# Mixer buffers and the first expert loads in another order, a gather in another place, and norms that take sums from their additions

## The reference

```python
h = layer_norm(x, ln_in_g, ln_in_b)
for l in range(DEPTH):                                    # DEPTH = 2
    y = token_mixers(h, l, ...)       # projections, 3 kinds of attention, gates, w_out
    h = layer_norm(ALPHA * h + y, ln_mix_g[l], ln_mix_b[l])
    if l % 2 == 0:
        y = swiglu(h, w_gate_dense, w_up_dense, w_down_dense)       # D_FF = 3584
    else:
        y = moe_ffn(h, ...)           # top 2 of 8 experts, each a SwiGLU of D_FF = 3584
    h = layer_norm(ALPHA * h + y, ln_ffn_g[l], ln_ffn_b[l])
```

## Time and profile before

| what | value |
|---|---|
| median of 3 runs (lowest, highest) | 1542.59 us (1541.73, 1545.37) |
| profiled execution: its own time, its span | 1543.59 us, 1540.9 us |
| granted TensorE clock, mean | 0.988 |
| PE, DVE, ACT busy | 1454.1, 763.5, 578.1 us |
| DMA | 473.71 MB, mean 307 GB/s |
| chain that ended last | PE 76%, DMA 17%, DVE 5% |
| second mixer's last matmul, item 0's first | 696.8 us, 716.95 us |
| item 2 begins, last item's last `down` ends | 898 to 902 us, 1521.9 us |

### The profile page before, as it was taken

The page is one execution under the profiler, slowest core; times in us unless marked ns, Lnnn a source line. Parts: engine busy times, 40 slices in busy tenths (PEclk is TensorE's granted clock), DMA queues, the critical chain, the costliest instruction groups (busy, mean ns, idle before and its releaser), DMA issues.

```text
span 1540.9 us, 17591 instructions
## 1 busy us (share of the span) xinstructions
PE 1454.1 (94%) x7442; PEld 999.9 (65%) x7442; DVE 763.5 (50%) x809; ACT 578.1 (38%) x605; POOL 13.3 (1%) x18
## 2 busy tenths in 40 slices
PE   8999999999999999999998789999987899999875
PEld 7988887888887988886342358873433588734222
DVE  7448687555547548674111059951010599510103
ACT  4357654343334357651000047740000477400001
POOL 1000000000000000010000000000000000000000
PEclk9999999999999999999999999999999999999998
DMA  9253265555544353259999999999999999999994
GB/s 349 106 224 121 99 246 194 182 191 191 186 169 164 110 219 123 96 218 398 431 430 429 430 429 431 430 396 432 429 430 431 428 430 430 396 430 431 429 428 178
DMA packets 42958, 473.71 MB, mean 307 GB/s; under 512 B 5392, under 2 KB 5520, under 8 KB 7424
## 3 DMA queue, kind: packets, MB, share of 16 engines
q1 hardware_dynamic: 42048, 467.97, 74.8%
q0 software_dynamic: 832, 4.63, 0.8%
HBM read 471.53 MB, written 1.05 MB: 307 GB/s over the span
## 4 chain that ended last, share of the span: by engine, by line
PE 76%; DMA 17%; DVE 5%; issue 1%; ACT 1%; SPq 0%; DVEq 0%; ACTq 0%
PE ps L1773 17%; PE ps L1774 17%; PE ps L1775 17%; DMA raw_a<-in_w_item 13%; PE ps L2189 12%; PE ps L2223 5%; DMA raw_b<-in_w_item 4%; PE ps L2149 2%; PE ps L1972 1%; PE ps L1939 1%; PE ps L2196 1%; PE ps L1809 1%; PE ps L1803 1%; PE ps L1962 1%; DVE small L1150 1%
## 5 line engine op out<-in xcount | busy, mean ns | idle before, releaser
L1134 DVE TENSOR_TENSOR lo_a<-raw_a,w_hi 128x2048 fp32r<-128x2048 f32 (+1 forms) x109 | 240.1, 2211 | 127.2 <-ACT w_hi L776 126.6
L1773 PE MATMUL ps<-w_hi,act_hi 128*128 128x512 f32 (+1 forms) x640 | 247.2, 386 | 1.4 <-DVE act_lo L1203 1.3
L776 ACT ACTIVATE w_hi<-raw_a 128x2048 fp32r<-128x2048 f32 (+1 forms) x109 | 200.6, 1848 | 120.4 <-PE ps L1775 120.4
L1775 PE MATMUL ps<-w_hi,act_lo 128*128 128x512 f32 (+1 forms) x640 | 243.5, 380 | 0.0
L1774 PE MATMUL ps<-lo_a,act_hi 128*128 128x512 f32 (+1 forms) x640 | 243.5, 380 | 0.0
L2189 PE MATMUL ps<-raw_a,x_small 128*64 128x512 f32 (+1 forms) x736 | 153.7, 568 | 16.0 <-DMA raw_a<-in_w_item 16.0
L2189 PE MATMUL ps<-raw_b,x_small 128*64 128x512 f32 (+1 forms) x800 | 147.6, 518 | 13.5 <-DMA raw_b<-in_w_item 13.5
L1049 ACT ACTIVATE hidT<-ps 128x512 f32<-128x512 f32 (+1 forms) x24 | 13.1, 544 | 335.7 <-PE ps L2196 335.7
L1773 PEld LDWEIGHTS ps<-w_hi,act_hi 128*128 128x128 f32 x640 | 121.5, 190 | 25.2 <-issue 2.2
L1775 PEld LDWEIGHTS ps<-w_hi,act_lo 128*128 128x128 f32 x640 | 121.0, 189 | 23.3
L1774 PEld LDWEIGHTS ps<-lo_a,act_hi 128*128 128x128 f32 x640 | 121.2, 189 | 21.6
(11 more groups left out here) (266 smaller groups left out, 1903.2 us busy)
## 6 DMA issues: line engine op xcount, KB each, us to landing
raw_b<-in_w_item SPq DMA_DIRECT2D x84, 2048.0 KB, 24.6
raw_a<-in_w_item SPq DMA_DIRECT2D x83, 2048.0 KB, 23.4
raw_a<-in_w_mix SPq DMA_DIRECT2D x60, 1024.0 KB, 5.0
raw_a<-in_w_item SPq DMA_DIRECT2D x44, 1024.0 KB, 5.1
raw_a<-in_w_mix SPq DMA_DIRECT2D x8, 512.0 KB, 3.7
ln_gb<-in_ln_mix POOLq DMA_DIRECT2D x2, 1024.0 KB, 5.0
cst<-in_consts SPq DMA_DIRECT2D x1, 1210.5 KB, 17.2
h<-in_x SPq DMA_DIRECT2D x2, 512.0 KB, 4.6
```

The source lines that it names most:

```text
L776: nc.scalar.activation(w_upper(g)[:, 0:n], raw(slot)[:, 0:n], ACT.Copy).then_inc(s_hi, 1)
L1134: nc.vector.tensor_tensor(w_lo(slot)[:, 0:n], raw(slot)[:, 0:n], w_upper(g)[:, 0:n].bitcast(F32), ALU.subtract).then_inc(s_lo, 1)
L1773: nc.tensor.matmul(dst, xh, wh, start=start, stop=False)
L1775: return nc.tensor.matmul(dst, xl, wh, start=False, stop=stop)
```

## The change

Four parts. (1) Item 0's units take the slots in the order `FIRST_SLOTS`, and each pair waits for what really last used its bytes; to this end the mixer's buffers are laid out anew (`gates` lowest, then `sb_tmp`, `wT`, `v_sb`, and `qkT` last), and two further slots 16 and 17 (`raw_x`, the second and third quarter of `w_hi`) are used once. (2) In S items `gather` stands behind `down(1)`; ScalarE's `copy_tokens` then waits until `project(3, up)` is done, whose input it overwrites. (3) Norms 1 and 2 become `boundary_norm`: the additions give row sums (`accum_out`), and ScalarE squares the deviations with a sum (`deviation_root`). Norm 3 stays. (4) The last norm does the same with the last `add_item`'s additions, with one root for both tiles.

```diff
+FIRST_SLOTS = (10, 11, 2, 3, 4, 5, 8, 9, 12, 13, 6, 7, 0, 1, 16, 17, 14, 15)
+RING = tuple(slot for slot in FIRST_SLOTS if slot < SLOTS)
...
-    k = (g - MOE_BASE) % SLOTS
-    return (MOE_BASE + k) % 8 if k < 8 else k
+    k = g - MOE_BASE
+    return FIRST_SLOTS[k] if k < len(FIRST_SLOTS) else RING[(k - len(FIRST_SLOTS)) % SLOTS]
...
+                elif slot == 10:
+                    sp.wait_ge(s_pv, DEPTH * 6)
+                    sp.wait_ge(s_rms, DEPTH * 2)
+                elif slot == 8:
+                    sp.wait_ge(s_used, MIX_BASE[DEPTH - 1] + U_OUT)
+                elif slot == 16:
+                    sp.wait_ge(s_used, max(HI_LAST[1:3]) + 1)
                 else:
-                    sp.wait_ge(s_used, MOE_BASE)
-                    if slot == SLOTS - 2:
+                    sp.wait_ge(s_mrg, DEPTH * 4)
+                    if slot == 14:
                         sp.wait_ge(s_lnd, 2 * DEPTH)
...
+            def deviation_root(t):
+                means[0] += 1
+                act.wait_ge(s_mn, means[0])
+                link(nc.scalar.activation(gates[:, 0, 0, :], h[:, t, :], ACT.Square, bias=minus_mean[:, t:t + 1],
+                                          accum_out=spread[:, t:t + 1]))
+                nc.scalar.activation(rr[:, 0:1], spread[:, t:t + 1], ACT.Sqrt, scale=1.0 / D, bias=tiny).then_inc(s_rr, 1)
...
+                    act.wait_ge(s_used, it.unit(it.of.up[3] + it.of.units[3]))
                     copy_tokens(it.n + 1, it.x_big(), it.next_banks())
...
+                def normalise_sums(t):
+                    link(nc.vector.tensor_scalar(minus_mean[:, t:t + 1], half_sums[:, 2 * t:2 * t + 1], half_sums[:, 2 * t + 1:2 * t + 2],
+                                                 -1.0 / D, ALU.add, ALU.mult))
+                    dve.sem_inc(s_mn, 1)
+                    for cols in halves:
+                        nc.vector.scalar_tensor_tensor(cat[:, t, cols], h[:, t, cols], minus_mean[:, t:t + 1], ln_gb[:, 0, cols],
+                                                       ALU.add, ALU.mult)
+                    dve.wait_ge(s_rr, seeds[0] + 1)
+                    link(nc.vector.tensor_scalar(rv[:, 0:1], spread[:, t:t + 1], 1.0 / D, 1e-5, ALU.mult, ALU.add))
+                    refine(1, rn[:, 0:1])
...
                 down(1)
+                if not it.big:
+                    gather(it.n + 1, it.x_big(), it.next_banks())
                 turn_hidden(2)
...
                 project(3, it.of.up[3], 2)
-                if not it.big:
-                    gather(it.n + 1, it.x_big(), it.next_banks())
                 down(2)
```

More of the change, by code:

```diff
@@ L462, in build @@
         s_raw = [sem(f"raw_loaded_{s}") for s in range(SLOTS_A)]
-        s_pair = [sem(f"pair_loaded_{s}") for s in range(SLOTS // 2)]
+        s_pair = [sem(f"pair_loaded_{s}") for s in range(SLOTS // 2 + 1)]
         s_last = sem("last_unit_loaded")
@@ L1116, in _ @@
             copy_down_hi(Item(STATIC_ITEMS - 1, n_loop))
-            root(1)
-            root(1)
+            for t in range(TILES):
+                act.wait_ge(s_mn, means[0] + t + 1)
+                link(nc.scalar.activation(x_rt[:, 0:4, :].rearrange("p k s -> p (k s)"), cat[:, t, :], ACT.Square,
+                                          bias=minus_mean[:, t:t + 1], accum_out=spread[:, t:t + 1]))
+            nc.scalar.activation(rr[:, 0:TILES], spread, ACT.Sqrt, scale=1.0 / D, bias=tiny).then_inc(s_rr, 1)
         @block.vector
@@ L1163, in normalise, with boundary_norm @@
                                                    ALU.mult, ALU.add).then_inc(s_h, 1)
+            def boundary_norm(n, params, arrive, turned, between=None, behind=None):
+                halves = [slice(0, 512), slice(512, 1024)]
+                def normalise_sums(t):
[8 more added lines that the diff above has]
+                    refine(1, rn[:, 0:1])
+                    for cols in halves:
+                        nc.vector.scalar_tensor_tensor(h[:, t, cols], cat[:, t, cols], rn[:, 0:1], ln_gb[:, 1, cols],
+                                                       ALU.mult, ALU.add).then_inc(s_h, 1)
+                for half in range(2):
+                    arrive(0, half)
+                dve.wait_ge(*params)
+                normalise_sums(0)
+                if between:
+                    between()
+                for half in range(2):
+                    turned(half)
+                    arrive(1, half)
+                normalise_sums(1)
+                if behind:
+                    behind()
+                turned(2)
+                turned(3)
+                dve.wait_ge(s_h, norm_done(n, TILES - 1, 1))
+                dve.sem_inc(s_lnd, 1)
             def norm(n, src, gb, params, arrive, turned=None, between=None, behind=None):
@@ L1761, in _ @@
             copy_down_lo(last)
[L1762 to L1767, removed]
+            weight = column(item_cw, last.col)
+            for t in range(TILES):
+                for half in range(2):
+                    dve.wait_ge(s_cb, last.n * 4 + (2 * t + half + 1))
+                    part_y = cat[:, t, 512 * half:512 * half + 512]
+                    link(nc.vector.scalar_tensor_tensor(part_y, ps[:, SCATTER_BANKS[2 * t + half], :], weight(t), part_y,
+                                                        ALU.mult, ALU.add, accum_out=half_sums[:, 2 * t + half:2 * t + half + 1]))
+                link(nc.vector.tensor_scalar(minus_mean[:, t:t + 1], half_sums[:, 2 * t:2 * t + 1], half_sums[:, 2 * t + 1:2 * t + 2],
+                                             -1.0 / D, ALU.add, ALU.mult))
+                dve.sem_inc(s_mn, 1)
+            dve.wait_ge(s_gbl, 16)
+            halves = [slice(0, 512), slice(512, 1024)]
+            for t in range(TILES):
+                for cols in halves:
+                    ins = nc.vector.scalar_tensor_tensor(h[:, t, cols], cat[:, t, cols], minus_mean[:, t:t + 1], ln_gb_last[:, 0, cols],
+                                                         ALU.add, ALU.mult)
+            link(ins)
+            dve.wait_ge(s_rr, seeds[0] + 1)
+            link(nc.vector.tensor_scalar(rv[:, 0:TILES], spread, 1.0 / D, 1e-5, ALU.mult, ALU.add))
+            refine(TILES, rn[:, 0:TILES])
+            for t in range(TILES):
+                for cols in halves:
+                    nc.vector.scalar_tensor_tensor(h[:, t, cols], h[:, t, cols], rn[:, t:t + 1], ln_gb_last[:, 1, cols],
+                                                   ALU.mult, ALU.add).then_inc(s_h, 1)
         @block.tensor
```

48 lines of the change are left out of this document (33 added, 15 removed).

## The result

The changed kernel takes 1527.99 us, the median of 4 runs (1527.33 to 1531.6), the kernel before beside it 1542.16 (4 runs). The ratio is 0.9909, 95% interval 0.9896 to 0.9923. The profiled execution took 1528.21 us, its span is 1526.3: 14.6 us less than the span of before.

A forecast was written before the change was run, and what follows sets the result against it. The items were taken to be bound by the weight stream, what comes before not. Gains of 8.5 + 0.9 + 2.3 + 3.2 = 14.9 us took the profiled 1543.59 to 1528.7, the median to 1527.7; range 1524 to 1534.

The forecast's parts named there:

- The upper bound of 1531: Whole kernel: top of the 1525.3 to 1531 us given for the forecast's own case, which had chance 0.70.
- Part 1, loads: Item 0's first weight loads: nine pairs go before TensorE begins, the tenth lands earlier; 8.5 us gained, between 7.9 and 9.2.
- The spare time: DMA before the tenth pair's issue at 720.64 us: idle 4 us, so the first nine waits could come that much later.
- largely idle: DMA engines between 662 and 694 us in the kernel before: said to lack slots that SyncE believes free.
- Part 2, gather: Last item, the only place with the gather on the path: without it there `down(3)` starts at 1517.3, not 1518.20; 0.9 us.
- Part 3, norms 1 and 2: VectorE's path in both norms: 1.04 us less per norm, plus 0.17 us of TensorE's wait in norm 1; 2.3 us.
- The accumulator's read: VectorE, behind each addition with a row sum: 0.10 us, taken from ScalarE's 187 ns instruction, about half overlapped.
- additions with a sum take twice as long: Rival, VectorE's additions in norms 1, 2 and the last: they would save nothing, total 1532.3 us; chance 0.10.
- Part 4, last norm: Kernel's end, first addition to last result: 10.5 us instead of 13.7, so 3.2 us less.
- the clock in the DMA-bound stretches: Slower rival, TensorE without the gather's filler: clock could fall, a pair taking 7.3 us instead of 3.65; chance 0.03.
- the stream's gain is not given back: Rival was that it is: TensorE overruns its spare time in items 0 and 1, total 1536.2 us; chance 0.10.
- the norms don't act alone: Rival was that only they act: early loads do not go early, up to 8.5 us less gain, 1536; chance 0.03.

The follow-up runs named there:

- kernel before with rounded places: Kernel before with one edit, the mixer's buffers beginning at a multiple of 64 bytes (32 bytes later): 1542.74 us, ratio 1.000.
- warm kernel: Changed kernel with 10 and 5 added keep-warm matmuls in the two gaps of TensorE's router stretch: 1524.93 us, ratio 0.9875.
- kernel with the third norm: Changed kernel with norm 3, ahead of the router, also in the new form (squares into `prob_odd`): 1528.19 us, ratio 0.9892.

## Why the prediction was right

1527.7 was predicted and 1528.0 measured; the sum of 14.9 us stands against 14.6 between the spans. The terms agree less well than the sum, and part of the agreement is luck. The upper bound of 1531 does not follow from the terms named for it, which add up to 1529.3, or 1530.0 with the accumulators at 0.19 us.

*Part 1, loads.* Predicted 8.5, bounds 7.9 to 9.2. From the release to item 2's first unit: 177.50 us before (720.64 to 898.14), 169.66 after: 7.8. The mechanism holds: nine pairs in by the release, an idle queue, a tenth pair that lands 7.7 us after its issue. A first pair 15.2 us later costs 1.0 us, and a pair fewer costs a pair. The spare time was put too low, at 4 us: it is 7.4, since the step from an idle queue's 7.5 to the 4.88 us of a full one was left out. And between 662 and 694 us the engines of the kernel before were not largely idle: their share there is 0.58.

*Part 2, gather.* Predicted 0.9, measured 1.0 (25.05 less 24.06), and right in mechanism: `down(2)`'s second pair now waits 1.17 us for data. It starts 19.49 us behind the second half of `down(1)`, which is four landings of 4.87 us each, as the prediction had them.

*Part 3, norms 1 and 2.* Predicted 2.3. Norm 1 gave 1.5 (first addition to last result 15.97 us before, 14.51 after), norm 2 gave 1.1: 2.6, by the traces; the medians of the kernel with the old norms do not show it. The accumulator's read, for which no row stood, was estimated at 0.10 us: it is a row of 0.08, and the next operation starts 0.73 us after the addition's start. By the Trainium skill ("VectorE: DVE Perf Modes", Two Vector instructions with no wait between them) this is two instructions, and the trace agrees. That additions with a sum take twice as long is refuted.

*Part 4, last norm.* Predicted 3.2, measured 2.7. The step that failed is "four additions 2.73, four accumulators 0.4, chaining 0.16, two small operations 0.4", 3.7 us; it is 4.3 (1512.82 to 1517.11). An addition from PSUM starts 0.89 us after the one before it, and behind the operation that hands on the mean VectorE idles 0.34 and 0.16 us: in the boundary norms I had counted handoffs, here not. The rest, 6.7 us, is as predicted.

*What I didn't have.* Ahead of the stream the release came 3.98 us earlier and not 2.3. Start and norms make 3.2 of it (0.67 us of start scatter), the dense stage's pace 1.8, the mixer behind it some 0.6, and the router's lower clock takes some 1.6 away. Behind item 2 the stream up to the last item's `down(1)` took 0.9 us more than before (595.88 against 595.02), which is within its scatter. So 3.1 us of gain (0.7, 1.8 and 0.6) and 2.5 us of loss (1.6 and 0.9) were in no term, and they nearly cancel: the four terms as measured sum to 14.1 us, with the rest 14.7. Either side alone would have put the forecast 2.5 to 3 us off, still inside its range.

I looked for the clock in the DMA-bound stretches, where TensorE waits 1.2 us at a time and stays at full clock as predicted; it fell at a gap of 1.49 us that was there before too (1.48), where the profile of before shows 3.37 us for the same matmuls. I don't know why that profile was spared. All eleven others without filler in the gap show the fall (0.50 to 0.88 in the window 696 to 702 us). One of them is that of the kernel before with rounded places (0.88), and there the fall costs nothing, because its DMA queue is full: the release comes 0.38 us later than in the kernel before (721.02 against 720.64), and item 2's first unit is split 0.91 us earlier all the same (897.23 against 898.14). The Trainium skill ("TensorE: Matmul & The Clock Gate", What's actually happening) says that idleness lowers the clock, and the warm kernel's trace agrees.

The rivals: the stream's gain is not given back (11.8 us of spare are left before item 2), the norms don't act alone, and item 2's matmuls wait 5.44 us instead of 4.81 (4.87 with the old gather) at the same granted 0.50.

## What to carry to other kernels

When a load stream bounds the end, count the pairs that can be in before its first release, and then look for the hole: if there is one, the compute ahead of the release has become the path again, and every microsecond there (a norm, filler matmuls, a clock that fell) counts, which it did not while the queue was full. No length of a wait told here where the clock falls (a lone one of 0.94 us did it, waits of 1.2 us at every pair did not), so read the granted clock behind each wait on the path. Filler matmuls are sized to the gap they fill: read what they take from the trace, and take some away when the work they cover gets shorter. To price an edit in a long stream, measure from a landing just ahead of it and not from the start. Undo each edit alone before trusting a sum that fits: here unseen gains and losses nearly cancelled.

## What the hardware showed that I had not expected

A gap of 1.49 us in TensorE's work, after full activity (90.00 of 90 us busy at 1.00 from 600 to 690 us in the changed kernel), let the granted clock fall to between 0.50 and 0.88 over the window 696 to 702 us in ten of eleven profiles. A gap of 0.94 us in the kernel with the third norm did so too (0.65) and kept it at 0.51 up to 714 us; item 2 then began 4.6 us later (891.01 against 886.45). ScalarE's square with a bias and a sum takes 1.15 us for 1024 columns where the earlier trace rows has 1.07 for an operation of this shape without, and its accumulator's read 0.18. And the place of a stationary operand in SBUF changes the pace of otherwise equal matmuls: 33.65 against 33.86 us for a block of the dense stage.
